# Conditioning sums in four column groups of one PSUM bank, and the latent half of context block 1 moved into the opening

## What is computed

```python
mod = jax.nn.silu(c) @ w_mod + b_mod              # (1, 12288); the first 4096 columns: shift, scale
sh1, sc1, g1, sh2, sc2, g2 = jnp.split(mod, 6, axis=-1)
mod_c = jax.nn.silu(c_ctx) @ w_mod[:, :4096] + b_mod[:4096]
shc, scc = jnp.split(mod_c, 2)
h  = rms_norm(x,   norm_mix_pre) * (1 + sc1) + sh1
hc = rms_norm(ctx, norm_mix_pre) * (1 + scc) + shc
p  = h  @ w_in                                    # 11296 columns
pc = hc @ w_in[:, :N_CTX_COLS]                    # the first 3616 columns (keys, values, gates)
...                                               # retention, gated linear attention, merge, w_out, SwiGLU
```

## Time and profile before

| | us |
|---|---|
| median of 3 runs | 1763.7 (1757.69 to 1764.57) |
| the profiled execution, its own time | 1764.71 |
| its span, first to last instruction | 1763.0 |
| last conditioning slot lands | 111.9 |
| block 1 begins / ends | 132.1 / 175.6 |
| mean granted TensorE clock | 0.993 of 2.4 GHz |

### The profile page before, as it was taken

How to read it: one execution, slowest core, us unless ns; L and a number is a source line. 1 busy time by engine, 2 the same in 40 slices (tenths; PEclk the granted TensorE clock), 3 DMA queues, 4 the chain that set the end, 5 groups by cost and what they waited for, 6 DMA issues and landing times.

```text
span 1763.0 us, 21644 instructions
## 1 busy us (share of the span) xinstructions
PE 1723.6 (98%) x7853; PEld 1387.9 (79%) x7853; DVE 982.3 (56%) x1073; ACT 737.4 (42%) x826; POOL 163.1 (9%) x180
## 2 busy tenths in 40 slices
PE   6999999999998999999999989999999999999998
PEld 3458888887877888888888868888888888888886
DVE  2346666648755676675565564444444444444444
ACT  3232222216654544454544474444444444443442
POOL 0010000000044453340000000000000000000000
PEclk9999999999999999999999999999999999999999
DMA  9999998869987666565777566666666666766662
GB/s 366 387 385 346 345 326 310 303 217 340 327 299 242 190 209 191 170 203 157 242 227 261 175 200 193 187 188 187 190 190 189 190 188 188 259 195 193 193 192 94
DMA packets 181674, 415.88 MB, mean 236 GB/s; under 512 B 12830, under 2 KB 13118, under 8 KB 171760
## 3 DMA queue, kind: packets, MB, share of 16 engines
q1 hardware_dynamic: 156288, 304.14, 54.5%
q10 hardware_dynamic: 17856, 82.43, 12.7%
q0 software_dynamic: 7472, 28.53, 4.8%
HBM read 394.55 MB, written 20.50 MB: 235 GB/s over the span
## 4 chain that ended last, share of the span: by engine, by line
PE 87%; DMA 5%; DVE 2%; issue 2%; ACT 2%; POOL 1%; SPq 0%; DVEq 0%; POOLq 0%; ACTq 0%
PE ps L1491 26%; PE ps L1495 26%; PE ps L1503 26%; DMA raw<-in_w_in 3%; PE ps L1752 1%; PE ps L1768 1%; ACT w_hi L605 1%; PE ps L1565 1%; DMA raw<-in_w_mod 1%; PE ps L1806 1%; PE ps L1548 1%; DMA xn<-in_x 1%; PE ps L1537 1%; DMA wm<-in_w_mod 0%; POOL dmat L437 0%
## 5 line engine op out<-in xcount | busy, mean ns | idle before, releaser
L1001 DVE TENSOR_TENSOR w_lo<-raw,w_hi 128x1024 fp32r<-128x1024 f32 x496 | 613.1, 1238 | 536.8 <-ACT w_hi L605 536.7
L605 ACT ACTIVATE w_hi<-raw 128x1024 fp32r<-128x1024 f32 x496 | 525.5, 1061 | 818.5 <-PE ps L1503 787.1
L1491 PE MATMUL ps<-w_hi,h_hi 128*128 128x512 f32 x1504 | 477.1, 397 | 1.8 <-DVE h_lo L1397 1.8
L1495 PE MATMUL ps<-w_hi,h_lo 128*128 128x512 f32 x1504 | 468.2, 391 | 0.0
L1503 PE MATMUL ps<-w_lo,h_hi 128*128 128x512 f32 x1504 | 413.0, 390 | 0.0
L1495 PEld LDWEIGHTS ps<-w_hi,h_lo 128*128 128x128 f32 x1504 | 283.6, 189 | 59.6
L1503 PEld LDWEIGHTS ps<-w_lo,h_hi 128*128 128x128 f32 x1504 | 283.5, 188 | 59.4
L1491 PEld LDWEIGHTS ps<-w_hi,h_hi 128*128 128x128 f32 x1504 | 280.5, 189 | 59.8 <-DVE h_lo L1397 2.5
L1013 DVE SCALAR_TENSOR_TENSOR acc<-wm,csil,acc 128x2048 f32<-128x2048 f32 (+1 forms) x60 | 141.0, 2350 | 92.5 <-DMA wm<-in_w_mod 92.5
L1491 PE MATMUL ps<-w_hi,hid_hi 128*128 128x512 f32 x352 | 109.7, 389 | 0.0
L1495 PE MATMUL ps<-w_hi,hid_lo 128*128 128x512 f32 x352 | 109.7, 389 | 0.0
(11 more groups left out here) (288 smaller groups left out, 1274.1 us busy)
## 6 DMA issues: line engine op xcount, KB each, us to landing
raw<-in_w_in SPq DMA_DIRECT2D x176, 512.0 KB, 5.3
wm<-in_w_mod ACTq DMA_DIRECT2D x64, 1024.0 KB, 6.8
raw<-in_ffn_w_gate SPq DMA_DIRECT2D x88, 512.0 KB, 4.4
raw<-in_ffn_w_up SPq DMA_DIRECT2D x88, 512.0 KB, 4.3
raw<-in_ffn_w_down SPq DMA_DIRECT2D x88, 512.0 KB, 4.6
raw<-in_w_mod SPq DMA_DIRECT2D x64, 512.0 KB, 8.5
raw<-in_w_out SPq DMA_DIRECT2D x32, 512.0 KB, 4.7
px<-stage ACTq DMA_DIRECT2D x44, 256.0 KB, 6.6
```

The source lines that it names most:

```text
L605: act.activation(w_hi[:, j % SPLIT, :, :], raw[:, j % RAW, :, :], ACT.Copy).then_inc(w_high, 1)
L1001: dve.tensor_tensor(w_lo[:, j % SPLIT, :, :], raw[:, j % RAW, :, :], w_hi[:, j % SPLIT, :, :].bitcast(F32), ALU.subtract).then_inc(w_low, 1)
L1491: pe.matmul(o, hi[:, kk, c], w_hi[:, q, e, :], start=kk == 0, stop=False)
L1495: pe.matmul(o, lo[:, kk, c], w_hi[:, q, e, :], start=False, stop=False)
```

## The change

1. Conditioning sums: k-tile k goes to column group k % 4, always in bank 6; `mod_row` has 128 partitions; the transposes are 128 wide and go to bank 7 only. A block's sums may start when the block before is copied out. Banks 4 and 5 are free for:
2. The latent half of context block 1 (columns 512 to 1023, `lat_part`, 12 matmuls a slot) runs in the opening, one slot a period. Its eight weight slots enter SP's list. The context half of block 1 stays behind the opening, in banks 6 and 7, with the same weights loaded and split a second time.
3. Context block 0 starts at period 2 instead of 3. Conditioning slots now come in pairs on PE: after slot 1 of a block stand the transposes and the last third of the context slot before, after 3 the latent slot, after 5 and 7 two thirds of the next context slot. `turn_x` stands behind slots 1, 3, 5, 7 of block 1 instead of 0, 2, 4, 6. Context slots 6 and 7 take the w_lo products ahead of the h_lo ones.
4. The chunks of the other conditioning columns: 2 in block 1, 46 over the 40 slots of blocks 2 to 6 (six slots have two). The loops of ACT and DVE over these blocks are written out.

```diff
@@ -57,7 +57,10 @@
 OUT_BLOCKS = D // N
 RAW, SPLIT = 8, 4
 MOD_BLOCKS = 8
-CTX_LAG = 3
+CTX_LAG = 2
+LATE_PAIRS = 6
+OPEN_SLOTS = 16
+OPEN_CHUNKS = 2
...
-                if j == 0 and n >= CTX_LAG:
+                if j == 2 and n >= CTX_LAG:
                     opening.append(("ctx", n - CTX_LAG))
-                if n == MOD_BLOCKS - 1 and j >= 5:
-                    opening.append(("ctx", j))
+                if j == 0 and n > CTX_LAG:
+                    opening.append(("lat", n - CTX_LAG - 1))
+        opening += [("lat", 5), ("ctx", 6), ("lat", 6), ("ctx", 7), ("lat", 7)]
...
+        def open_number(what):
+
+            return 2 * what[1] + (what[0] == "lat")
+
+        def chunks_at(b, j):
+
+            if b == 1:
+                return range(j // 4, j // 4 + 1) if j % 4 == 3 else range(0)
+            t = 8 * (b - 2) + j
+            first, more = OPEN_CHUNKS + t * 46 // 40, OPEN_CHUNKS + (t + 1) * 46 // 40
+            return range(first, more)
...
                 if isinstance(s, int) and j < len(opening) + SPLIT - 1:
-                    act.wait_ge(w_used, j - len(opening) + SPLIT + 1)
+                    act.wait_ge(w_used, j - len(opening) + OPEN_SLOTS - SPLIT + 1)
...
             def take_mod_row(n):
                 act.wait_ge(S("mod_used"), 8 * (n + 1))
-                act.activation(mod_row[:, n, :], bank(4 + n % 2)[0:3 * GROUP, :], ACT.Copy).then_inc(S("mod_row_ready"), 1)
+                act.activation(mod_row[:, n, :], bank(6), ACT.Copy).then_inc(S("mod_row_ready"), 1)
...
             for n in range(1, MOD_BLOCKS):
+                if n >= CTX_LAG:
+                    split_open("ctx", n - CTX_LAG)
+                take_mod_row(n)
+                if n >= CTX_LAG:
+                    split_open("lat", n - CTX_LAG)
                 if n == MOD_BLOCKS - 1:
-                    split_ctx(5)
-                    split_ctx(6)
-                take_mod_row(n)
-                if 2 <= n < MOD_BLOCKS - 1:
-                    split_ctx(n - 2)
-                if n == MOD_BLOCKS - 1:
-                    split_ctx(7)
+                    split_open("ctx", 6)
                 if n % 2 == 1:
                     high_pair(2 * n - 2)
                     high_pair(2 * n)
+            split_open("lat", 6)
+            split_open("ctx", 7)
+            split_open("lat", 7)
             act.wait_ge(S("mod_cols_done"), MOD_BLOCKS)
             load_chunk(0, 0, 0, 0)
...
+            for b in range(1, CTX_BLOCKS):
+                for j in range(8):
+                    if j == 4:
+                        stage_ctx(b - 1, (b - 1) % 2)
+                    if j == 5:
+                        store_ctx(b - 1)
+                    split(S_CTX + 8 * b, j)
+                    for n in chunks_at(b, j):
+                        load_chunk(0, n + 1, *chunk_of(n + 1))
...
             for n in range(1, MOD_BLOCKS):
-                if n == MOD_BLOCKS - 1:
-                    split_ctx(5)
-                    split_ctx(6)
+                if n >= CTX_LAG:
+                    split_open("ctx", n - CTX_LAG)
                 if n % 2 == 1:
                     modulate(n // 2)
                     scale_pair(dve, 2 * n - 2, "h1_ready")
                     scale_pair(dve, 2 * n, "h1_ready")
-                    if n == MOD_BLOCKS - 1:
-                        split_ctx(7)
+                    if n >= CTX_LAG:
+                        split_open("lat", n - CTX_LAG)
                     low_pair(dve, 2 * n - 2, "h1_lo")
                     low_pair(dve, 2 * n, "h1_lo")
                 else:
                     mod_columns(n)
-                if n < MOD_BLOCKS - 2:
-                    split_ctx(n - 1)
-            for j in range(8):
-                split(S_CTX + 8, j)
-                add_chunk(0, j, 0, j)
-            dve.wait_ge(S("consts_landed"), 16 * 5)
-            dve.tensor_copy(mask[:, :, :], mask_f[:, :, :]).then_inc(S("mask_ready"), 1)
-            with dve.Fori(0, 2) as i:
-                for u in range(2):
-                    for j in range(8):
-                        n = 8 + 8 * u + j
-                        add_chunk(i, n, *chunk_of(n))
-                        split(i * 16 + (S_CTX + 16 + 8 * u), j)
-            for j in range(8):
-                add_chunk(0, 40 + j, *chunk_of(40 + j))
-                split(S_CTX + 48, j)
+                    if n >= CTX_LAG:
+                        split_open("lat", n - CTX_LAG)
+            for kind, i in (("ctx", 6), ("lat", 6), ("ctx", 7), ("lat", 7)):
+                split_open(kind, i)
+            for b in range(1, CTX_BLOCKS):
+                if b == 2:
+                    dve.wait_ge(S("consts_landed"), 16 * 5)
+                    dve.tensor_copy(mask[:, :, :], mask_f[:, :, :]).then_inc(S("mask_ready"), 1)
+                for j in range(8):
+                    for n in chunks_at(b, j):
+                        add_chunk(0, n, *chunk_of(n))
+                    split(S_CTX + 8 * b, j)
...
-                if n == 1:
+                if n == 0:
                     pe.wait_ge(S("cols_ready"), 3)
-                if n >= 2:
-                    pe.wait_ge(S("mod_ready"), n - 1)
+                else:
+                    pe.wait_ge(S("mod_ready"), n)
                 for r in range(4):
-                    last = pe.transpose(bank(6 + n % 2)[:, r * 3 * GROUP:(r + 1) * 3 * GROUP],
-                                        mod_row[:, n, r * P:(r + 1) * P], ident[0:3 * GROUP, 0:3 * GROUP])
+                    last = pe.transpose(bank(7)[:, r * P:(r + 1) * P], mod_row[:, n, r * P:(r + 1) * P], ident[:, :])
...
-                    g = (n + k) % 3
-                    last = pe.matmul(bank(4 + n % 2)[g * GROUP:(g + 1) * GROUP, :], c_pad[:, k, :],
-                                     raw[:, place % RAW, e, :], start=k < 3, stop=k >= KT - 3,
+                    g = k % 4
+                    last = pe.matmul(bank(6)[g * GROUP:(g + 1) * GROUP, :], c_pad[:, k, :],
+                                     raw[:, place % RAW, e, :], start=k < 4, stop=k >= KT - 4,
                                      tile_position=(0, g * GROUP))
                 last.then_inc(S("mod_used"), 1)
...
-                q, k, e = i % SPLIT, 2 * i, r % 2
+                o, late = open_number(("ctx", i)), i >= LATE_PAIRS
+                q = o % SPLIT
+                if late:
+                    steps = (((0, h_hi, hc_hi, w_hi), (1, h_hi, hc_hi, w_hi)),
+                             ((0, h_hi, hc_hi, w_lo), (1, h_hi, hc_hi, w_lo)),
+                             ((0, h_lo, hc_lo, w_hi), (1, h_lo, hc_lo, w_hi)))[r]
+                elif r < 2:
+                    steps = ((r, h_hi, hc_hi, w_hi), (r, h_lo, hc_lo, w_hi))
+                else:
+                    steps = ((0, h_hi, hc_hi, w_lo), (1, h_hi, hc_hi, w_lo))
                 if r == 0:
+                    pe.wait_ge(S("h1_hi" if late else "h1_lo"), i + 1)
+                    pe.wait_ge(w_high, o + 1)
+                if r == (1 if late else 2):
+                    pe.wait_ge(w_low, o + 1)
+                if r == 2 and late:
                     pe.wait_ge(S("h1_lo"), i + 1)
-                    pe.wait_ge(w_high, i + 1)
+                for a, (e, h, hc, w) in enumerate(steps):
+                    for n, (t, m) in enumerate(((h, 0), (h, 1), (hc, 0), (hc, 1))):
+                        last = pe.matmul(bank(n), t[:, 2 * i + e, m * P:(m + 1) * P], w[:, q, e, :],
+                                         start=i == 0 and r == 0 and a == 0, stop=i == 7 and r == 2 and a == 1)
                 if r == 2:
-                    pe.wait_ge(w_low, i + 1)
-                for a, w in ((0, w_hi), (1, w_hi)) if r < 2 else ((0, w_lo), (1, w_lo)):
-                    for n, (hi, lo, m) in enumerate(CTX):
-                        kk, c = k + (e if r < 2 else a), slice(m * P, (m + 1) * P)
-                        h = lo if r < 2 and a == 1 else hi
-                        last = pe.matmul(bank(n), h[:, kk, c], w[:, q, kk - k, :], start=kk == 0 and r < 2 and a == 0,
-                                         stop=r == 2 and kk == KT - 1)
-                if r == 2:
-                    last.then_inc(w_used, 1 if i < 7 else 1 + 8 * MOD_BLOCKS)
+                    last.then_inc(w_used, 1)
+
+            def lat_part(i):
+
+                o = open_number(("lat", i))
+                q = o % SPLIT
+                pe.wait_ge(S("h1_lo"), i + 1)
+                pe.wait_ge(w_high, o + 1)
+                for a, (e, t, w) in enumerate(((0, h_hi, w_hi), (0, h_lo, w_hi), (1, h_hi, w_hi), (1, h_lo, w_hi),
+                                               (0, h_hi, w_lo), (1, h_hi, w_lo))):
+                    if a == 4:
+                        pe.wait_ge(w_low, o + 1)
+                    for m in range(MT):
+                        last = pe.matmul(bank(4 + m), t[:, 2 * i + e, m * P:(m + 1) * P], w[:, q, e, :],
+                                         start=i == 0 and a == 0, stop=i == 7 and a == 5)
```

(29 more changed lines are left out.)

58 lines of the change are left out of this document (17 added, 41 removed).

## The result

The forecast was 1757.5 us. The changed kernel takes 1767.6 us (median of 17 runs, 1760.8 to 1774.9), the kernel before 1758.5 beside it (17 runs, 1757.3 to 1767.2): ratio 1.0039, 95% interval 1.0024 to 1.0055. It is 0.4% slower. The time lies 1.6 us above my range, and the sign is wrong.

What follows compares the result with a forecast made beforehand. TensorE was taken to bound the kernel, except in the opening, where DMA sets the pace. An earlier end of block 1, -7.2 us, and buffer gaps, +1.0, gave -6.2 from 1763.7: 1757.5 us, range 1751.5 to 1766.

Steps and rivals of the forecast that it cites:

- Pair of conditioning slots: Opening: four matmuls, one in each of four column groups, cost TensorE 0.985 us, bounds 0.98 and 1.85.
- rival (a): Opening: the fourth column group does not run beside the others, a pair costs 1.85 us; 1774 us, slower; chance 0.12.
- Period 13.51 us by DMA, 13.48 by TensorE: Each of five new opening periods: ten slot loads against TensorE's matmuls and transposes, level, DMA setting the pace.
- The ring of eight raw buffers: Opening: DVE frees some slots 7.1 to 7.3 us after landing, opening DMA gaps; +1.0 us, 0 to 4.
- The start: Opening's first stretch: times taken over from the kernel before, with no term for a difference.
- The tail: After the last transposes: TensorE waits 2.65 us for latent slot 5 and 0.9 for context slot 6; opening ends at 146.7.
- Block 1's half: Context half of block 1 behind the opening: eight slots of 12 matmuls take 21.75 us, ending at 168.4.
- Behind block 1: Blocks 2 to 6: 9.2 chunks per full block cost nothing thanks to DVE's lead; 0 us, bounds 0 and +3.
- Later waits: TensorE's later waits are few, the longest 4.6 us for the sums through HBM, and keep their order; 0, within 2.
- Rival (b): The opening slips: slower pairs 1.3 us, DMA gaps 4, doubled chunks 3; 1760 to 1765 us; chance 0.18.

Runs made afterwards that it cites:

- early splits: Changed kernel with DVE's splits of latent slots moved ahead of the scaling and of context slots ahead of the low parts; 1758.3 us, 0.9979 of the kernel before.
- early latent slots only: Changed kernel with only the latent slots' DVE splits moved ahead of the scaling, context slots unchanged; 1761.6 us, 1.0009 of the kernel before.
- the one of 5794.7 us: A profiled execution of the changed kernel with latent and context splits moved forward; it took 5794.7 us, stands in no comparison, and that kernel was run again.
- other chunk plan: Changed kernel with four chunks in block 1, 44 over blocks 2 to 6, DVE's split between a double slot's additions; 1762.3 us, 1.0008 of the kernel before.
- three groups: Changed kernel with three column groups in the one bank instead of four for the conditioning sums; 1782.1 us, 1.0132 of the kernel before.
- periods only: Changed kernel with DVE's latent and context splits moved forward in the opening's periods, period 7 and tail unchanged; 1761.8 us, 0.9995 of the kernel before.
- period 7 only: Changed kernel with DVE's splits of latent slot 5 and context slot 6 moved forward, earlier periods unchanged; 1763.8 us, 1.0006 of the kernel before.
- early with the other plan: Changed kernel with early splits and the other chunk plan together, nothing left out; 1754.5 us, 0.9950 of the kernel before.

## Why the prediction was wrong, step by step

- *Pair of conditioning slots, 0.985 us:* right, 1.00, which disposes of rival (a). The rule of the Trainium skill ("TensorE: Matmul & The Clock Gate", "Step-by-step: what each phase is for") on the fourth quadrant did not bite here; the four 32-column tiles of "TensorEngine Tiling (Array Packing)", "Tiling Modes", do run side by side.
- *Period 13.51 us by DMA, 13.48 by TensorE:* right as bounds. The kernels with early splits reach 13.5 to 13.6 in their undisturbed periods.
- *The ring of eight raw buffers, +1.0 us (0 to 4):* **the step that failed.** The last transposes were to start at 123.5 plus this term, and started at 130.0. The kernel with early splits, whose execution is level with the changed one when period 2 opens (transposes at 43.09 and 43.12), has them at 125.12: the term measured 4.9 us. I had the limit right (a buffer must come free within 10.8 - 3.8 = 7.0 us of its landing) but put the release at 7.1 to 7.3; it is 7.6 for latent slot 1 and 8.0 for context slot 0 (split at 50.91; it landed at 42.9 by an estimate, two slots of 1.35 us ahead of conditioning slot 4, for which TensorE waited until 45.58). And I priced a miss at its shortfall, 0.1 to 0.3 us, where each of the three dips cost 1.3 to 2.0: once the queue is empty the engines also stand through the start of the next transfer. In the first dip SyncE issues at 50.93, and the changed kernel's windows say:

```profile
50.00:51.00 1.00, 1.00 (x7) 0.79 (x5) 0.91 (x1) 0.00 (x0) 0.00 (x0) 1.00 0.19 68
51.00:52.00 1.00, 1.00 (x8) 0.34 (x9) 0.00 (x0) 0.00 (x0) 0.00 (x0) 1.00 0.06 23
...
52.50:53.00 0.50, 0.50 (x6) 0.42 (x3) 0.00 (x0) 0.30 (x1) 0.00 (x0) 1.00 0.65 180
53.00:53.50 0.50, 0.50 (x4) 0.41 (x3) 0.00 (x0) 0.50 (x2) 0.00 (x0) 1.00 0.97 377
```

  Some 2 us pass from the issue to the first full slice. The Trainium skill ("DMA: Bandwidth & Descriptors", "Anatomy of one DMA — SWDGE (gpsimd) path") gives about 2 us fixed for a transfer issued by GpSimd, most of them behind the last byte; here SyncE issues and the time stands ahead of the full rate, so the trace agrees with the size and not with the place. I had used that figure only as a duration, not as the price of letting the queue run dry. The three dips add up to 4.8 us of DMA time, about the whole term.
- *The start, no term:* I took the first 42 us over from the kernel before. There the transposes that open period 2 start at 42.07, in the changed kernel at 43.12. TensorE's granted clock was 0.50 (1.2 GHz) from 24 to 32 us while it turned x; where it was 1.00 from 30 us on, as in the kernel with early latent slots only, they start at 41.65. The executions of these kernels differ in this from one to the next, by some 1.5 us, and nothing was run on the cause.
- *The tail, waits of 2.65 and 0.9 us:* the first is there with 2.75. The second is not, since TensorE came late to it: the clock of 0.57 behind the first wait, 1.5 us, was missing from the sum. Tail 24.2 us against 23.2. That the clock can fall with a stop was to be read from the kernel before, whose granted clock was 0.63 and 0.52 in the windows 20 to 24 and 24 to 28 us, in and behind a stop of 7.0 us; I had not put that question. The Trainium skill ("TensorE: Matmul & The Clock Gate", "Part 1: The HAM clock gate") says that idling does it, and the tail agrees; the stops of 2.34 and 3.37 us named above had no such stretch, so the length of a stop alone does not tell.
- *Block 1's half 21.75 us:* right, 21.76.
- *Behind block 1, 0 (0 to +3):* **failed too**, 4.3 us. I took the price of 0 from DVE's lead of three slots and from the bandwidth, 343 of 387 GB/s. Neither is the limit: the stream has only two buffers, and its own period (5 to 12 us of landing plus 2.36 of addition for two chunks in flight) was level with the demand. A wait that costs nothing, 92.5 us of it on DVE, is no proof of reserve.
- *Later waits, 0 within 2, "keep their order":* in the profiled executions the stretch behind the gates gave 1.1 us back, inside the bounds. Over all runs the step **failed**: the changed kernel is in the upper group in 14 of 17 runs and the kernel before in 5, and this takes the difference from 3.3 us within a group to 9.1 between the medians. The cause stays open.

The sum: -6.2 + 5.5 (last transposes at 130.0 instead of 124.5; 3.9 of it by the ring, the rest mostly by the start) + 1.0 (tail) + 4.3 (chunks) - 1.1 = +3.5 us, the difference of the spans. Rival (b), with 0.18, was what happened in two of its three parts: its sizes (4 us of gaps, 3 of chunks) were each exceeded, its slower pair did not come. The base was off as well: I took the median of three runs, 1763.7, and the median of 17 is 5 us lower. I had forecast -6.2 us; the runs gave +3.3 within a group and +9.1 between the medians.

## What to carry to other kernels

When a change brings two limits level, the queue order behind them becomes the limit: follow, for the buffer that the issuing engine comes to next and not for the one that is held longest, who frees it, and price a dry queue at the full restart of a transfer (here 1.3 to 2.0 us a time), not at the shortfall. Before a stage of two profiled executions is compared, look where they already differ ahead of the edit: here 1.5 us stood there. A stream through two buffers has a period of its own, and doubling its demand in a few slots can cost more than the average shows; spread it, and put the urgent work between. TensorE's stops in a dense stretch can cost more than their length, through the clock behind them.

## What the runs showed of the chip beside this

The two groups of runs differ behind the gates. From the gate product to the end it is 1326.2 to 1326.6 us in three of the profiled executions and 1331.8 to 1333.7 in the ten others (the one of 5794.7 us left out). The likely cause is a race of GpSimd and DVE: behind the gates GpSimd builds the decay tables and then sends the conditioning sums through HBM (sumd); TensorE waits for them. GpSimd's and DVE's rows in the kernel before, then in the one with the other chunk plan, whose profiled execution is of the lower group:

```profile
516.68 1.34 DVE L1001 TENSOR_TENSOR w_lo<-raw,w_hi 128x1024 fp32r<-128x1024 f32 x1 [5.29 <-ACT w_hi L605]
517.04 2.42 POOL L435 TENSOR_SCALAR d_tmp<-dist,lg 128x512 f32<-128x512 f32 x1
...
543.94 0.37 PE L1661 MATMUL ps<-ident,rows 64*128 64x64 f32 x1 [4.56 <-DMA rows<-sumd]
```

```profile
517.55 1.57 POOL L451 TENSOR_SCALAR d_tmp<-dist,lg 128x512 f32<-128x512 f32 x1
517.87 1.45 DVE L1004 TENSOR_TENSOR w_lo<-raw,w_hi 128x1024 fp32r<-128x1024 f32 x1 [5.28 <-ACT w_hi L621]
...
541.14 0.27 PE L1695 MATMUL ps<-ident,rows 64*128 64x64 f32 x1 [0.55 <-DMA rows<-sumd]
```

Where DVE is first by 0.36 us, GpSimd's operation takes 2.42 us and ends 1.44 us behind DVE's, as if it had begun only then; where GpSimd is first, 1.57. Longer and shorter operations of GpSimd follow one another from there, the sums leave 105.2 or 101.5 us behind the gate product, and TensorE waits 4.4 to 5.0 or 0.5 to 0.6 us. Behind the long wait its granted clock was 0.50 (1.2 GHz) in the kernel before and 0.57 in the changed one for some 4 us, behind the short one 1.00 (2.4 GHz): some 4 us of wait and, by an estimate from these two windows, 1.6 to 3 us of clock. Every profile above is of one kind or the other; in three the wait is short (three groups, early latent, other plan). The Trainium skill ("GPSIMD Engine Reference", "Key points") says that GpSimd shares its SBUF interfaces with DVE and gets in the way of DVE instructions with two inputs in SBUF, as the split has; the durations agree. That this one race decides the group is not shown: in three kernels (periods only, period 7 only, early with the other plan) GpSimd is first at this place (1.57 us), and the sums still leave 105.2 us behind the gate product, after a first operation that began 84.4 to 85.2 us behind it instead of 82.2 to 83.6; and no kernel has a profile of each group. Why the changed kernel is in the upper group more often (14 of 17 runs against 5) was not tried and stays open.
